# Latent attention by pairs of heads in a hybrid encoder trunk: rotary scores as two 64-row tiles

## The reference

```python
q = (rms_norm(q_lat, q_lat_norm) @ w_q_up).reshape(B, S, H, MLA_QK)      # H = 4, MLA_QK = 128 + 64
kv = (rms_norm(kv_lat, kv_lat_norm) @ w_kv_up).reshape(B, S, H, MLA_NOPE + MLA_V)
k = concat([k_nope, broadcast(k_rope)]);  q, k = rms_norm(q), rms_norm(k)
q, k = [nope part, rotary(rope part)]                                     # 128 and 64 features
s = einsum('bqhd,bkhd->bhqk', qb, k) * scale                              # blocks of 128 queries
s = where(key_chunk <= q_chunk, s, MASK_VALUE)                            # chunks of 64
out = einsum('bhqk,bkhd->bqhd', softmax(s), v)
```

## Time and profile before

| | |
|---|---|
| median of 3 runs | 1375.46 us |
| the profiled execution | 1374.74 us, span 1373.0 us |
| PE busy | 1357.8 us (99%) |
| DVE, ACT, POOL busy | 958.8, 705.6, 516.0 us |
| granted TensorE clock | full over the whole span |

### The profile page before, as it was taken

The page is one execution under the profiler, slowest core; times in us unless marked ns, Lnnn a source line. Parts: engine busy times, 40 slices in busy tenths (PEclk is TensorE's granted clock), DMA queues, the critical chain, the costliest instruction groups (busy, mean ns, idle before and its releaser), DMA issues.

```text
span 1373.0 us, 19396 instructions
## 1 busy us (share of the span) xinstructions
PE 1357.8 (99%) x7551; PEld 1128.6 (82%) x7551; DVE 958.8 (70%) x1380; ACT 705.6 (51%) x1170; POOL 516.0 (38%) x327
## 2 busy tenths in 40 slices
PE   8999999999999999999999999999999999999999
PEld 6888778887879988998988887788778888888887
DVE  4583773665889569857985657836658895797587
ACT  6747483665444344434466465835754433434333
POOL 5745665642430222032036456655335203220420
PEclk9999999999999999999999999999999999999999
DMA  6332112331471475066133220133325706741641
GB/s 181 100 91 74 31 47 79 122 108 49 150 200 47 144 194 138 17 177 154 22 92 93 86 77 16 48 97 118 92 62 169 198 17 177 191 107 39 189 95 61
DMA packets 180923, 142.58 MB, mean 104 GB/s; under 512 B 15169, under 2 KB 153184, under 8 KB 180832
## 3 DMA queue, kind: packets, MB, share of 16 engines
q1 hardware_dynamic: 175664, 124.55, 30.3%
q0 software_dynamic: 4608, 16.78, 6.4%
q10 hardware_dynamic: 560, 0.01, 0.0%
HBM read 122.44 MB, written 2.10 MB: 91 GB/s over the span
## 4 chain that ended last, share of the span: by engine, by line
PE 92%; DVE 4%; ACT 2%; DMA 1%; issue 1%; POOL 0%; SPq 0%; DVEq 0%; POOLq 0%
PE bank L770 27%; PE bank L772 27%; PE bank L771 27%; PE bank L944 2%; PE bank L1101 1%; PE bank L1102 1%; PE bank L1087 1%; PE bank L932 1%; DMA w_lo<-raw 1%; PE bank L1254 1%; PE bank L1169 1%; DVE scores_h L2181 1%; DMA x_tok<-in_x 1%; PE bank L1011 1%; DVE Q L2164 0%
## 5 line engine op out<-in xcount | busy, mean ns | idle before, releaser
L690 POOL TENSOR_TENSOR w_lo<-raw,w_hi 128x1024 fp32r<-128x1024 f32 (+3 forms) x148 | 360.0, 2437 | 642.0 <-ACT w_hi L1370 640.4
L770 PE MATMUL bank<-x_hi,w_hi 128*128 128x512 f32 x944 | 371.8, 394 | 4.0 <-DMA w_lo<-raw 1.9
L771 PE MATMUL bank<-x_lo,w_hi 128*128 128x512 f32 x944 | 367.7, 390 | 0.0
L772 PE MATMUL bank<-x_hi,w_lo 128*128 128x512 f32 x944 | 367.7, 389 | 0.0
L1370 ACT ACTIVATE w_hi<-raw 128x1024 fp32r<-128x1024 f32 (+2 forms) x181 | 189.4, 1047 | 125.5 <-PE bank L772 124.8
L770 PEld LDWEIGHTS bank<-x_hi,w_hi 128*128 128x128 f32 x944 | 177.2, 188 | 47.5 <-issue 8.0
L771 PEld LDWEIGHTS bank<-x_lo,w_hi 128*128 128x128 f32 x944 | 177.3, 188 | 37.2 <-issue 1.4
L772 PEld LDWEIGHTS bank<-x_hi,w_lo 128*128 128x128 f32 x944 | 177.2, 188 | 37.0
L771 PE MATMUL bank<-p_lo,w_hi 128*128 128x256 f32 x308 | 87.3, 283 | 0.0
L772 PE MATMUL bank<-p_hi,w_lo 128*128 128x256 f32 x308 | 87.3, 283 | 0.0
L770 PE MATMUL bank<-p_hi,w_hi 128*128 128x256 f32 x308 | 87.2, 283 | 0.0
(11 more groups left out here) (351 smaller groups left out, 2766.0 us busy)
## 6 DMA issues: line engine op xcount, KB each, us to landing
raw<-in_w_ffn_in SPq DMA_DIRECT2D x88, 512.0 KB, 4.2
w_lo<-raw POOLq DMA_DIRECT2D x32, 512.0 KB, 4.8
raw<-in_w_in SPq DMA_DIRECT2D x27, 512.0 KB, 3.8
raw<-in_w_mix_out SPq DMA_DIRECT2D x16, 512.0 KB, 3.9
raw<-in_w_ca_kv SPq DMA_DIRECT2D x32, 256.0 KB, 3.4
b_y<-in_w_ffn_out SPq DMA_DIRECT2D x10, 512.0 KB, 5.8
b_x<-in_w_ffn_out SPq DMA_DIRECT2D x10, 512.0 KB, 5.3
b_z<-in_w_ffn_out SPq DMA_DIRECT2D x10, 512.0 KB, 5.5
```

The costliest lines, as they stand in the source:

```text
L690: pool.tensor_tensor(w_lo[gi % SPLIT][:, c0:n], whole[:, c0:n], w_hi[gi % SPLIT][:, c0:n].bitcast(f32), ALU.subtract).then_inc(S["lo_split ...
L770: pe.matmul(o, ah, bh, start=first, stop=False, skip_group_check=shared_bank)
L771: pe.matmul(o, ah, bl, start=False, stop=False, skip_group_check=shared_bank)
L772: mm = pe.matmul(o, al, bh, start=False, stop=last, skip_group_check=shared_bank)
```

## The change

PE, DVE and ACT get a loop of their own for the latent attention. Items are now ordered by pairs of heads: `mla_item(i)` gives heads 2p and 2p+1 alternately for one token group, then the next group. At an even step PE writes the scores of two items, into banks 0 and 1: first the non-rotary matmuls of both heads, then the rotary ones, in which the two heads use rows 0 to 63 and rows 64 to 127. `qT_r` has only two slots without zeros (the memsets go), and one ACT copy replaces two. `probsT` becomes four buffers, one an item, and the output product is done per pair of heads and token group at odd steps, both heads side by side in bank 3; its high and low parts are copied for both heads at once. The second diagonals move from step 7 to step 8. Buffers are placed anew.

```diff
-        probsT = place("probsT", R0, [P, NT, SEQ])
+        probsT = [place(f"probsT{i}", R0 + 2 * i, [P, SEQ]) for i in range(4)]
-        qT_r = place("qT_r", R1 + 16, [P, NH, SEQ])
-        kT_r = place("kT_r", R3, [P, 2, SEQ])
+        qT_r = place("qT_r", R1 + 16, [P, 2, SEQ])
+        kT_r = place("kT_r", R1 + 20, [P, 2, SEQ])
...
+        MLA_PV = MLA_ITEMS // 2
+        def mla_item(i):
+            pair, g = divmod(i // 2, len(MLA_GROUPS))
+            return 2 * pair + i % 2, MLA_GROUPS[g]
...
-                        if i == SPLIT - 1:
-                            for half in range(2):
-                                pool.memset(qT_r[:, 2 * half:2 * half + 2, :], 0.0).then_inc(S["zeroed"], 1)
...
+                    def latent_attention(between):                                  # PE
+                        for i in range(MLA_ITEMS + 4):
+                            if i < MLA_ITEMS and i % 2 == 0:
+                                hd, ts = mla_item(i)
+                                spans, c = [], 0
+                                for t in ts:
+                                    spans.append((slice(t * P, (t + 1) * P), slice(c, c + (t + 1) * P), (t + 1) * P))
+                                    c += (t + 1) * P
+                                for a in range(2):
+                                    claim(a)
+                                    for q, o, n in spans:
+                                        pe.matmul(pb[a][:, o], qT_n[:, hd + a, q], kT_n[:, hd + a, 0:n], start=o.start == 0, stop=False, skip_group_check=True)
+                                for q, o, n in spans:
+                                    last = []
+                                    for a in range(2):
+                                        r = slice(ROPE * a, ROPE * (a + 1))
+                                        last.append(pe.matmul(pb[a][:, o], qT_r[r, hd // 2, q], kT_r[r, hd // 2, 0:n], start=False, stop=o.stop == c, skip_group_check=True))
+                                for a in range(2):
+                                    mark(last[a], S["score_mm"])
+                                    freed[a] = (S["score_exp"], past(layer, "score_exp") + i + a + 1)
+                            j = i - FLIGHT
...
+                            j = i - 4
+                            if 0 <= j and j % 2:
+                                claim(3)
+                                pe.wait_ge(S["probsT_evac"], past(layer, "probsT_evac") + j + 1)
+                                for a in range(2):
+                                    hd, ts = mla_item(j - 1 + a)
+                                    w = len(ts) * P
+                                    for n in range(ts[-1] + 1):
+                                        q0 = max(0, n - ts[0]) * P
+                                        mm = pe.matmul(pb[3][:, 256 * a + q0:256 * a + w], v_tok[:, n, hd * VD:(hd + 1) * VD], mla_probs(j - 1 + a)[:, n, q0:w],
+                                                       start=n == 0, stop=n == ts[-1])
+                                mark(mm, S["pv_mm"])
+                                freed[3] = (S["pv_lo"], past(layer, "pv_lo") + j // 2 + 1)
...
                     def dense_between(i):
+                        if i == 8:
+                            diagonals(1)
                         first = sum(CIG_UNITS.get(j, 0) for j in range(i))
...
-                        if i in (3, 7):
-                            diagonals(i == 7)
+                        if i == 3:
+                            diagonals(0)
...
-                            if z:
-                                ev = act_.activation(dr[:, :, t * P:(t + 1) * P], two, ACT.Copy)
-                            else:
-                                for r in range(2):
-                                    half = slice(ROPE * r, ROPE * (r + 1))
-                                    ev = act_.activation(dr[half, r::2, t * P:(t + 1) * P], two[half], ACT.Copy)
-                            ev.then_inc(S["qkT_evac"], 1)
+                            act_.activation(dr[:, :, t * P:(t + 1) * P], two, ACT.Copy).then_inc(S["qkT_evac"], 1)
```

More of the change, by code:

```diff
@@ L908, in token_group @@
                             freed[bs[t]] = (evac[0], evac[1] + t + 1)
+                    def latent_attention(between):
+                        for i in range(MLA_ITEMS + 4):
+                            if i < MLA_ITEMS and i % 2 == 0:
+                                hd, ts = mla_item(i)
+                                spans, c = [], 0
[15 more added lines that the diff above has]
+                            j = i - FLIGHT
+                            if 0 <= j < MLA_ITEMS:
+                                claim(2)
+                                pe.wait_ge(S["probs_done"], past(layer, "probs_done") + j + 1)
+                                for c in range(0, sum(t + 1 for t in mla_item(j)[1]) * P, P):
+                                    mm = pe.transpose(pb[2][:, c:c + P], probs[j % FLIGHT][:, c:c + P], ident[:, :])
+                                mark(mm, S["probsT_mm"])
+                                freed[2] = (S["probsT_evac"], past(layer, "probsT_evac") + j + 1)
+                            j = i - 4
[11 more added lines that the diff above has]
+                                freed[3] = (S["pv_lo"], past(layer, "pv_lo") + j // 2 + 1)
+                            between(i)
@@ L946, in attend @@
                                 mark(mm, S["pv_mm"])
-                                freed[b] = (S["pv_lo"], past(layer, "pv_lo") + base // MLA_ITEMS * NH + hd + 1)
+                                freed[b] = (S["pv_lo"], past(layer, "pv_lo") + MLA_PV + hd + 1)
                             between(i)
@@ L1096, in _ @@
                     pe.wait_ge(S["v_evac"], past(layer, "v_evac") + NT)
-                    pe.wait_ge(S["zeroed"], past(layer, "zeroed") + 2)
-                    def mla_score(o, hd, t, n):
-                        pe.matmul(o, qT_n[:, hd, t * P:(t + 1) * P], kT_n[:, hd, 0:n], start=True, stop=False)
-                        return pe.matmul(o, qT_r[:, hd, t * P:(t + 1) * P], kT_r[:, hd // 2, 0:n], start=False, stop=True)
-                    attend(0, MLA_BANKS, MLA_GROUPS, mla_score, lambda t: (t + 1) * P, lambda n: n * P,
-                           lambda n, hd: v_tok[:, n, hd * VD:(hd + 1) * VD], [probsT], probs, between=dense_between)
+                    latent_attention(dense_between)
                     mixed = [0]
```

117 lines of the change are left out of this document (95 added, 22 removed).

## The result

The changed kernel took **1379.7 us** (median of 6 runs, 1377.9 to 1380.58), the kernel before 1375.26 beside it (6 runs, 1374.12 to 1375.72): a ratio of 1.0036 on record, 95% interval [1.0026, 1.0046] (the two medians alone divide to 1.0032). That is slower, by more than the 0.2% that a measurement of this kernel tells. The profiled execution took 1379.98 us, its span 1378.3, 5.3 above that of before.

What follows compares the result with a forecast made beforehand. PE was taken to bound the kernel, busy 1357.8 of 1373.0 us. The terms sum to -0.3 us a layer, -0.6 in two, set against the median of 1375.46: 1374.9 us, range 1371.3 to 1380.3.

Steps and rivals of the forecast that it cites:

- no change: Likeliest case for the whole kernel: the terms nearly cancel, 1374.9 us, within the 0.2% a measurement tells; chance 0.45.
- slip at step 13: Rival: DVE slips one more POOL base, its negation falls into the weight split; wait 3.5 us, 1379.3 us; chance 0.29.
- two 64-row tiles overlap: Rotary scores: two heads on 64 rows each cost the time of one, saving 4.3 us a layer (bounds 0 to 4.3).
- six excursions: PE's switches into 64-row tiles and back, one per head pair and token group: 0.30 us each, +1.8 us a layer.
- output product's columns: 256 more columns of the output product stand ahead of the last transposes: +0.43 us a layer.
- shorter tail before the sweeps: Behind the last transposes, ACT's and DVE's last pieces for the sweeps halve: -0.40 us a layer.
- wait at step 6: PE wants score bank 1 at S+5.4, the exponential of item 5 frees it at S+6.3: +0.9 us a layer.
- wait at step 13: PE waits for ACT's copy of item 9's transposes, DVE being held by POOL's bases: 1.3 us, or 3.5 with a slip.
- granted clock behind that wait: PE's clock after the wait at step 13: the prediction counted no cost for it.
- behind the phase: After the phase, which runs from a layer's first score matmul to its last sweep matmul: no change counted.
- that is a tie without POOL: Step 13: PE wants the transpose bank at S+6.5, ACT's copy comes at S+6.3, before counting POOL's bases.
- near even, slightly for the hit: Step 13: whether DVE's maximum of item 10 ends less than 2.8 us before POOL's last base; 10.3 misses, 10.75 hits.

Runs made afterwards that it cites:

- e4: Changed kernel with each head's rotary matmuls over all 128 rows, so no 64-row tiles (scores not the reference's): 1381.64 us, ratio 1.0045 to the kernel before.
- e8: Changed kernel with both heads' rotary matmuls over rows 0 to 63, so no overlap (scores not the reference's): 1382.95 us, ratio 1.0058 to the kernel before.
- e6: Changed kernel with GpSimd's second set of score bases moved behind the two splits that follow it: 1373.7 us, ratio 0.9996 to the kernel before.
- e1: Changed kernel with ScalarE's cast of the first memory sum called one step later (12 instead of 11): 1376.16 us, ratio 1.0012 to the kernel before.
- e3: Changed kernel with four extra unread 128x512 float32 matmuls on PE ahead of the transposes of item 10: 1382.27 us, ratio 1.0052 to the kernel before.
- e10: On top of e5, ScalarE's two expansions of step 11 put behind the copy at that step's start, ahead of the exponential: 1369.85 us, ratio 0.9966 to the kernel before.
- e5: Changed kernel with dense units ahead of the transposes at odd steps from 5 and ScalarE's cast one step later: 1371.65 us, ratio 0.9979 to the kernel before.
- e7: Changed kernel with dense units first at odd steps, ScalarE's cast a step later and GpSimd's second bases behind the splits: 1380.43 us, ratio 1.004 to the kernel before.
- e9: On top of e5, ScalarE's two expansions of step 11 called at step 10: 1371.71 us, ratio 0.9979 to the kernel before.
- e11: On top of e10, VectorE's second product of the first queries called at step 5 instead of 4: 1372.82 us, ratio 0.9991 to the kernel before.

## Why the prediction was wrong

The likeliest case, no change, failed; the rival "slip at step 13" (0.29, 1379.3) came. Point by point, per layer:

| step of the prediction | forecast | found |
|---|---|---|
| two 64-row tiles overlap | -4.3 | -4.2 |
| six excursions | +1.8 | +2.1 (e4, e8: 6 x 0.35) |
| output product's columns | +0.43 | +0.45 (e6, e8: 6.68 against 6.23 us ahead of the sweeps) |
| shorter tail before the sweeps | -0.40 | -0.28 (25.23 to 24.95 us of sweeps) |
| wait at step 6 | +0.9 | +0.6 |
| wait at step 13 | +1.3, or 3.5 | +3.2 (gap 3.44 - 0.23) |
| granted clock behind that wait | none | +1.6 (e1, e8, e3) |
| not placed | | +0.3 |
| sum in the phase | -0.3 | measured 80.87 - 77.14 = +3.73 |
| behind the phase | 0 | -1.0 |

The found column is checked by e10: without the wait at step 13 and the clock, the placed terms come to -1.3, and its phase is 77.14 - 76.06 = 1.08 shorter, so the same part of about 0.3 is missing there. I can't place it; the transposes ahead of the sweeps take 0.4 us more even in e4, which has no 64-row tiles (3.67 against 3.28).

The shorter tail has the size forecast, roughly, but not the reason. The prediction said that ACT sets the pace there. In the kernel before PE idles for 0.2 us at most in a layer's sweeps, so PE sets the pace, and the gain is its own: the output product's passes among the sweeps take 1.88 instead of 2.25 us, the columns that went ahead.

**The step that failed** is the choice of 1.3 us for step 13, where "that is a tie without POOL" and "near even, slightly for the hit" had been worked out and the cheaper side was taken as likeliest. The working said that the slip decides when the maximum of item 10 ends less than 2.8 us before the last base does. In the trace after it ended at 165.01 and the last base at 167.60: 2.6, so the slip. The prediction's own count put 2.7 or 3.15 us between the two (13.1 or 13.55 less 10.4), one on either side of 2.8, and then gave the slip only 0.29. Its terms were good: behind the start of the second diagonals (154.66) the maximum ended 10.35 us later (10.4 forecast) and the last base 12.94 (13.1), because the bases took 11.05 and not 11.65. e6 shows the mechanism by removing it. The order of ACT's queue (e1, e5, e10) decides only how much of DVE's lateness reaches PE.

**What was missed** is the clock. The prediction had no row of a PE wait of this size inside busy stretches, put the clock at nothing without a reason, and counted a wait at its own length; here a wait of 3.2 cost 4.8. The overlap of the row tiles was the forecast where the Trainium skill spoke for less: TensorE: Matmul & The Clock Gate, section Measured speedup vs the span model, has 3.07 for four row tiles. The trace doesn't show that inefficiency inside a run of passes (starts 6 to 7 ns apart, and passes at the full rate); but a loss comes all the same, under another name, since an excursion loses 0.35 us at its edges, with or without overlap: 4.2 saved for 2.1 paid is a net 2.1, and the page's ratio for a short run of tiles may well hold such edges. That is argued, not shown.

**Behind the phase** about 1.0 us came back in each layer, which was not forecast. In both layers PE's spacing of 0.5 and 0.96 us among the products of the scores (L1169) is gone, and between the layers the transfers of w_lo (1.9 to 1.4 us) are waited for less. From the last sweep matmul of layer 1 to the end every variant takes 491.8 to 491.9 us, against 492.8 before; between the two phases all take 601.4 to 602.0 but e3 (602.7), against 603.0. e4 has it too, so it isn't the 64-row tiles. Which part of the change removes the stall at L1169 wasn't tried and stays open.

So 1379.7 is close to the rival's 1379.3 by errors that offset each other: over both layers +3.2 of clock, +0.6 of excursions, +0.2 of the tail, +0.2 of the overlap and +0.6 not placed against -2.0 behind the phase and -1.2 in the two waits. That is +1.6 and goes by the profiled executions, which are 5.3 us apart; the medians are 4.4 apart.

## What to carry to other kernels

A change that takes columns off TensorE moves every meeting with the engines that feed it; where a count ends in a near tie, take the loss to be as likely as the gain. Here the queue with the longest indivisible pieces decided it, GpSimd's products of 1.4 to 2.5 us beside VectorE's negations of 0.16. Look then for independent work that can stand ahead of the instruction that waits: moving the dense units of the odd steps, one cast and two expansions, with no work removed, turned +0.36% into -0.34%. Move one piece at a time and look at what stood behind it in its own queue, since e7, e9 and e11 each cured the wait that they were made for and made another.

## What the hardware showed that I had not expected

- PE's granted clock fell to 1.2 GHz behind a single wait and stayed there while PE was already working: 0.57 from 174 to 178 us. One such fall cost 1.6 us (e1, e8). In the profiled executions it fell in both layers behind PE's gaps of 3.44, 3.04 and 2.91 us, in one layer of two behind those of 2.49 and 2.54, and in no phase behind 2.08 and shorter ones. The gap alone doesn't decide: near the start of the program it fell in e3 and e11, at 12.8 and 13.2 us behind gaps of 1.7, and not in ten other executions, which have gaps of 1.5 to 1.7 there too. What else decides wasn't tried.
- Two 64-row tiles of float32 overlap fully, 6 to 7 ns apart; entering and leaving the shape costs 0.35 us, and starting two at once adds next to nothing. A pair of heads of 128+256 columns saves 0.64 for that 0.35.
- VectorE instructions with a few bytes of work took 1.2 to 1.4 us beside GpSimd's products, eight times their 0.16.
